# A decoder layer's conditioning products: from split fp32r weights to plain fp32 in two column strips

## The reference

```python
cs = jax.nn.silu(c)
ada = (cs @ w_ada[l] + b_ada[l]).reshape(B, N_ADA, D_MODEL)        # 1024 x 9216
h = modulate(rmsnorm(x, g_ffn1[l]), sh1, sc1)
x = x + 0.5 * gt1[:, None] * swiglu(h, w_ffn1_in[l], w_ffn1_out[l])
h = modulate(rmsnorm(x, g_mix[l]), sh2, sc2)
...
x = x + gt2[:, None] * out                                          # token mixer
h = modulate(rmsnorm(x, g_ffn2[l]), sh3, sc3)
x = x + 0.5 * gt3[:, None] * swiglu(h, w_ffn2_in[l], w_ffn2_out[l])
fin = cs @ w_ada_final + b_ada_final                                # 1024 x 2048
```

## Time and profile before

| what | value |
|---|---|
| time, median of three runs | 3044.75 us (3041.53 to 3051.48) |
| the profiled execution: span from first to last instruction | 3042.0 us |
| PE busy | 2895.1 us (95%) |
| PE weight loads busy | 2778.0 us (91%) |
| DVE busy | 1463.0 us (48%) |
| ACT busy | 867.4 us (29%) |
| mean granted TensorE clock (1 is full speed) | 0.974 |
| memory traffic | 63 GB/s over the span |

### The profile page before, as it was taken

How to read it: one execution, slowest core, us unless ns; L and a number is a source line. 1 busy time by engine, 2 the same in 40 slices (tenths; PEclk the granted TensorE clock), 3 DMA queues, 4 the chain that set the end, 5 groups by cost and what they waited for, 6 DMA issues and landing times. The chain is left out here.

```text
span 3042.0 us, 45017 instructions
## 1 busy us (share of the span) xinstructions
PE 2895.1 (95%) x17729; PEld 2778.0 (91%) x17729; DVE 1463.0 (48%) x3102; ACT 867.4 (29%) x1396; POOL 131.1 (4%) x190
## 2 busy tenths in 40 slices
PE   5899999999998989999999999999989999999997
PEld 3799999999998989889988988998889999999996
DVE  4655545444445644436345433634674443343436
ACT  5422222222213412332233233223441111111114
POOL 2000000000003010000000000000200000000002
PEclk7899999999999999999999999999999999999998
DMA  7122222222111131212111221211021111111111
GB/s 227 53 88 96 97 97 86 94 97 97 55 42 29 43 101 50 73 32 68 49 56 32 65 73 32 67 49 56 22 70 42 41 55 41 41 41 41 41 42 59
DMA packets 167528, 193.05 MB, mean 63 GB/s; under 512 B 7760, under 2 KB 157036, under 8 KB 167349
## 3 DMA queue, kind: packets, MB, share of 16 engines
q1 hardware_dynamic: 166962, 191.12, 19.7%
q10 hardware_dynamic: 342, 0.15, 0.0%
q0 software_dynamic: 96, 0.00, 0.0%
HBM read 172.38 MB, written 18.87 MB: 63 GB/s over the span
## 5 line engine op out<-in xcount | busy, mean ns | idle before, releaser
L521 DVE SCALAR_TENSOR_TENSOR xT<-ps,gate_p,xT 128x384 f32<-128x384 f32 (+1 forms) x624 | 348.3, 571 | 115.5 <-PE ps L801 97.4
L907 PE MATMUL ps<-hhi,mw_hi 128*128 128x384 f32 (+1 forms) x1152 | 392.6, 341 | 9.2 <-DVE mw_lo L1684 7.4
L908 PE MATMUL ps<-hlo,mw_hi 128*128 128x384 f32 (+1 forms) x1152 | 379.3, 329 | 0.0
L738 DVE TENSOR_TENSOR hf<-st,ps 128x384 f32<-128x384 f32 x132 | 70.2, 532 | 642.3 <-PE ps L822 640.3
L909 PE MATMUL ps<-hhi,mw_lo 128*128 128x384 f32 (+1 forms) x1152 | 378.9, 329 | 0.0
L820 PE MATMUL ps<-hhi,wa_hi 128*128 128x384 f32 (+1 forms) x1056 | 350.0, 331 | 16.9 <-DVE wa_lo L728 14.0
L821 PE MATMUL ps<-hlo,wa_hi 128*128 128x384 f32 (+1 forms) x1056 | 347.8, 329 | 0.0
L822 PE MATMUL ps<-hhi,wa_lo 128*128 128x384 f32 (+1 forms) x1056 | 347.5, 329 | 0.0
L820 PE MATMUL ps<-hhi,wb_hi 128*128 128x384 f32 (+1 forms) x1056 | 346.1, 328 | 0.1
L822 PE MATMUL ps<-hhi,wb_lo 128*128 128x384 f32 (+1 forms) x1056 | 346.0, 328 | 0.0
L821 PE MATMUL ps<-hlo,wb_hi 128*128 128x384 f32 (+1 forms) x1056 | 346.0, 328 | 0.0
(11 more groups left out here) (298 smaller groups left out, 5250.7 us busy)
## 6 DMA issues: line engine op xcount, KB each, us to landing
ada_raw<-in_w_ada SPq DMA_DIRECT2D x36, 1024.0 KB, 5.1
mw_raw<-in_w_in SPq DMA_DIRECT2D x32, 1024.0 KB, 5.7
wa_raw<-in_w_ffn_in SPq DMA_DIRECT2D x22, 1024.0 KB, 5.1
wb_raw<-in_w_ffn_in SPq DMA_DIRECT2D x22, 1024.0 KB, 5.2
wo_raw<-in_w_ffn_out SPq DMA_DIRECT2D x22, 1024.0 KB, 4.9
ada_raw<-in_w_ada_final SPq DMA_DIRECT2D x8, 1024.0 KB, 5.3
cs<-in_state_mlstm_C SPq DMA_DIRECT2D x32, 256.0 KB, 2.8
out_C_sample<-cs SPq DMA_DIRECT2D x32, 256.0 KB, 2.2
```

The costliest lines, as they stand in the source:

```text
L521: ins = dve.scalar_tensor_tensor(out=xT[:, m, t0:t0 + wp], in0=ps[:, bank, 0:wp], scalar=gate_p[:, m:m + 1], in1=xT[:, m, t0:t0 + wp], op0 ...
L738: dve.tensor_tensor(M["hf"][:, n, 0:w], M["st"][:, n, 0:w], ps[:, up_bank("b", b, i, n), 0:w], ALU.mult).then_inc(C["hidden"].sem, 1)
L907: pe.matmul(out, wh, xh, start=(j == 0), stop=False)
L908: pe.matmul(out, wh, xl, start=False, stop=False)
```

## The change

The products take the raw fp32 weights: the splits by ACT and DVE go, and with them the buffers `ada_hi` and `ada_lo`. silu(c) is kept as fp32, nine columns padded with zeros to 32 (`csT`). The eight matmuls of a group alternate between two strips of 32 columns of the array: even slices k add up in PSUM partitions 0 to 31, odd ones in 32 to 63. ACT copies 64 rows out, and the turn, before a pair of transposes, is a pair of plain fp32 matmuls against `strip_sum`, a 128 x 9 matrix of zeros and ones that adds the two strips. `ada_keep` is one operation. The memory of the split buffers serves as raw slots: ten in `bring_in` (loads 10 and 11 wait for products 0 and 1), two in `ffn`, where the load of a group waits for the product two before it.

```diff
+        ADA_FIRST, ADA_SLOTS = 12, 10
+        ada_raw = [ar.put(f"ada_raw{s}", [P, KT, 256]) for s in range(2)] + [
+            ar.put(f"ada_raw{s}", [P, KT, 256], at=hi_at + 8192 * (s - 2)) for s in range(2, ADA_SLOTS)]
+        ada_rows = ar.put("ada_rows", [P, 256])
+        strip_sum = ar.put("strip_sum", [P, 9])
+        csT = ar.put("csT", [P, KT, 32])
+        ar.at = top + 3 * 8192
...
-        def ada_high(act, turn, halves_free, slot=0, half=0):
-            act.wait_ge(*ada_in[slot](turn * 16 + 16))
-            if halves_free is not None:
-                act.wait_ge(*ada_mm(halves_free))
-            for i in range(2):
-                act.activation(ada_hi[half][:, :, 128 * i:128 * i + 128], ada_raw[slot][:, :, 128 * i:128 * i + 128],
-                               ACT.Copy).then_inc(ada_hi_done.sem, 1)
-        def ada_low(dve, g, slot=0, half=0):
-            for i in range(2):
-                c = slice(128 * i, 128 * i + 128)
-                dve.wait_ge(*ada_hi_done(g * 2 + (i + 1)))
-                dve.tensor_tensor(ada_lo[half][:, :, c], ada_raw[slot][:, :, c], ada_hi[half][:, :, c].bitcast(F32),
-                                  ALU.subtract).then_inc(ada_lo_done.sem, 1)
-        def ada_product(pe, g, half=0, reused=True):
-            pe.wait_ge(*ada_lo_done(g * 2 + 2))
+        def ada_product(pe, g, slot, turn, reused=True):
+            pe.wait_ge(*ada_in[slot](turn * 16 + 16))
             if reused:
                 pe.wait_ge(*ada_rows_kept(g))
             for k in range(KT):
-                pe.matmul(ps[0:18, 6, 0:256], cs_r[:, k, :], ada_hi[half][:, k, :], start=(k == 0), stop=False)
-                ins = pe.matmul(ps[0:18, 6, 0:256], cs_r[:, k, :], ada_lo[half][:, k, :], start=False, stop=(k == KT - 1))
+                strip = 32 * (k % 2)
+                ins = pe.matmul(ps[strip:strip + 32, 6, 0:256], csT[:, k, :], ada_raw[slot][:, k, :], start=(k < 2), stop=(k >= KT - 2))
             ins.then_inc(ada_mm.sem, 1)
         def ada_copy_rows(act, g, reused=True):
             act.wait_ge(*ada_mm(g + 1))
             if reused:
                 act.wait_ge(*ada_turned(g))
-            act.activation(ada_rows[:, :], ps[0:18, 6, 0:256], ACT.Copy).then_inc(ada_rows_kept.sem, 1)
+            act.activation(ada_rows[0:64, :], ps[0:64, 6, 0:256], ACT.Copy).then_inc(ada_rows_kept.sem, 1)
         def ada_turn(pe, g, reused=True):
             if reused:
...
             pe.wait_ge(*ada_rows_kept(g + 1))
             pe.sem_inc(ada_passed.sem, 1)
             for i in range(2):
-                ins = pe.transpose(ps[:, 7, 18 * i:18 * i + 18], ada_rows[:, 128 * i:128 * i + 128], ident[0:18, 0:18])
+                ins = pe.matmul(ps[:, 7, 9 * i:9 * i + 9], ada_rows[:, 128 * i:128 * i + 128], strip_sum[:, :], start=True, stop=True)
             ins.then_inc(ada_turned.sem, 1)
         def ada_keep(dve, g):
             dve.wait_ge(*ada_turned(g + 1))
             dst = ada[:, bass.ds(g * 2, 2), :]
-            out = ps[:, 7, 0:36].rearrange("p (j s) -> p j s", s=18)
-            dve.tensor_tensor(dst, out[:, :, 0:9], bc(bT[:, bass.ds(g * 2, 2)], 2, 9), ALU.add).then_inc(*dve_steps.one())
-            dve.wait_ge(*dve_steps.now())
-            dve.tensor_tensor(dst, dst, out[:, :, 9:18], ALU.add).then_inc(ada_kept.sem, 1)
+            out = ps[:, 7, 0:18].rearrange("p (j s) -> p j s", s=9)
+            dve.tensor_tensor(dst, out, bc(bT[:, bass.ds(g * 2, 2)], 2, 9), ALU.add).then_inc(ada_kept.sem, 1)
...
-                    for g in range(12):
-                        if g >= 4:
-                            sp.wait_ge(*ada_lo_done(2 * (g - 4) + 2))
-                        ada_load(sp, g, g % 4)
+                    for g in range(ADA_FIRST):
+                        if g >= ADA_SLOTS:
+                            sp.wait_ge(*ada_mm(g - ADA_SLOTS + 1))
+                        ada_load(sp, g, g % ADA_SLOTS)
...
-                    def high(g):
-                        ada_high(act, g // 4, g - 2 if g >= 3 else None, g % 4, g % 3)
                     for u, (t0, n) in enumerate(UNITS):
                         for k in range(1, KT, 2):
                             g = KT * u + k
                             act.wait_ge(*x_turned(g + 1))
                             act.activation(xT[:, k, t0:t0 + n], ps[:, g % 6, 0:n], ACT.Copy).then_inc(x_kept_a.sem, 1)
-                        high(u)
                         if u == 0:
                             act.wait_ge(*v_turned(1))
-                            act.activation(csT[:, :, :], ps[:, 6, 0:72], ACT.Copy).then_inc(v_kept.sem, 1)
-                            act.wait_ge(*v_kept(1))
-                            act.activation(cs_r[:, :, 0:9], csT[:, :, :], ACT.Copy).then_inc(v_kept.sem, 1)
+                            act.wait_ge(*made(5))
+                            act.activation(csT[:, :, 0:9], ps[:, 6, 0:72].rearrange("p (k s) -> p k s", s=9), ACT.Copy).then_inc(cs_ready.sem, 1)
                     act.wait_ge(*v_turned(2))
                     act.activation(bT[:, :], ps[:, 7, 0:ALL_T], ACT.Copy).then_inc(v_kept.sem, 1)
                     act.activation(vT[:, :], ps[:, 7, 128:256], ACT.Copy).then_inc(v_kept.sem, 1)
...
                     act.wait_ge(*x_kept_a(12))
                     for g in range(12):
                         ada_copy_rows(act, g, reused=g >= 1)
-                        if g < 9:
-                            high(g + 3)
                         sq.square(act, 2 * g)
                         sq.square(act, 2 * g + 1)
...
-                        ada_low(dve, u, u, u)
+                    dve.wait_ge(*made(6))
+                    dve.tensor_tensor(strip_sum[:, :], ident[:, 0:9], ident[:, 32:41], ALU.add).then_inc(made.sem, 1)
                     dve.wait_ge(*v_kept(2))
-                    dve.tensor_tensor(cs_r[:, :, 9:18], csT[:, :, :], cs_r[:, :, 0:9].bitcast(F32), ALU.subtract).then_inc(cs_ready.sem, 1)
-                    dve.wait_ge(*v_kept(4))
-                    for g in range(12):
-                        if g < 9:
-                            ada_low(dve, g + 3, (g + 3) % 4, g % 3)
-                        if g >= 1:
-                            ada_keep(dve, g - 1)
-                    ada_keep(dve, 11)
+                    for g in range(ADA_FIRST):
+                        ada_keep(dve, g)
...
-                            sp.wait_ge(*ada_lo_done(group(b, q) * 2))
-                            ada_load(sp, group(b, q))
+                            sp.wait_ge(*ada_mm(group(b, q) - 1))
+                            ada_load(sp, group(b, q), q % 2)
...
-                                ada_product(pe, group(b, 2 * i + n // 2))
+                                q = 2 * i + n // 2
+                                ada_product(pe, group(b, q), q % 2, b * 2 + (q // 2 - 2))
```

More of the change, by code:

```diff
@@ L145, in layer @@
         ar.at = top = ar.end // 32 * 32 - 4 * (RINGS * 384 + T + KT * NSEQ * STOK) - 3 * 8192
-        ada_raw = [ar.put("ada_raw0", [P, KT, 256])] + [
-            ar.put(f"ada_raw{s}", [P, KT, 256], at=hi_at + 8192 * (s - 1)) for s in range(1, 4)]
-        ada_hi = [ar.put("ada_hi0", [P, KT, 256], F32R), ar.put("ada_hi1", [P, KT, 256], F32R, at=hi_at + 3 * 8192),
-                  ar.put("ada_hi2", [P, KT, 256], F32R, at=hi_at + 5 * 8192)]
-        ada_lo = [ar.put("ada_lo0", [P, KT, 256], F32R), ar.put("ada_lo1", [P, KT, 256], F32R, at=hi_at + 4 * 8192),
-                  ar.put("ada_lo2", [P, KT, 256], F32R, at=hi_at + 6 * 8192)]
+        ADA_FIRST, ADA_SLOTS = 12, 10
[5 more added lines that the diff above has]
+        ar.at = top + 3 * 8192
         norm_at = ar.at
@@ L154, in layer @@
         rr = ar.put("rr", [P, T])
-        ada_rows = ar.put("ada_rows", [18, 256], at=ar.at)
         ts = ar.put("norm_samples", [P, KT, NSEQ, STOK])
-        ada_in = [cnt(f"ada_in{s}") for s in range(4)]
-        ada_hi_done, ada_lo_done, ada_mm, ada_rows_kept, ada_turned, ada_kept, ada_passed = (
-            cnt("ada_" + n) for n in ("hi_done", "lo_done", "mm", "rows_kept", "turned", "kept", "passed"))
+        ada_in = [cnt(f"ada_in{s}") for s in range(ADA_SLOTS)]
+        ada_mm, ada_rows_kept, ada_turned, ada_kept, ada_passed = (
+            cnt("ada_" + n) for n in ("mm", "rows_kept", "turned", "kept", "passed"))
         squared, squares_added, mean_done, rms_done, t_done, hi_done, lo_done = (
@@ L276, in bring_in @@
             crow2 = ar.put("crow2", [9, D])
-            csT = ar.put("csT", [P, KT, 9])
             brow = ar.put("brow", [ALL_T, P])
@@ L347, in _ @@
                     pool.memset(eps_col[:, :], EPS).then_inc(made.sem, 1)
-                    pool.wait_ge(*made(3))
+                    pool.memset(csT[:, :, :], 0.0).then_inc(made.sem, 1)
+                    pool.memset(ada_rows[:, :], 0.0).then_inc(made.sem, 1)
+                    pool.wait_ge(*made(5))
                     pool.affine_select(out=ident[:, :], in_=ident[:, :], compare_op=ALU.not_equal, fill=1.0,
@@ L396, in _ @@
```

(28 more changed lines are left out.)

6 lines of the change are left out of this document (1 added, 5 removed).

## The result

The changed kernel takes **3013.44 us** (median of four runs, 3009.16 to 3015.38) against 3047.23 (four runs, 3041.53 to 3051.48): a ratio of 0.9888, 95% interval 0.9868 to 0.9908, or some 34 us less. The profiled execution took 3013.23 us with a span of 3010.8 us, at a mean granted clock of 0.980.

What follows compares the result with a forecast made beforehand. PE's own work was taken to bound ffn, a chain of waits bring_in. ffn +12.8 and start -21.0 give -8.2 us on the profiled 3042.0, 3033.8; with 2.75 to the median, 3036.5 us, range 3026 to 3064.

Steps and rivals of the forecast that it cites:

- ffn, +12.8: First ffn: a group costs PE 2.79 us against 2.39, +0.40 for each of 32 groups.
- the start, -21.0: bring_in: last product starts at 63.1 us against 84.57, with a tail longer by 0.5.
- The sign named for the first: First ffn: PE busy over 719 of 720 us would confirm that ACT and DVE were covered there.
- staggered pairs: Each product: records of the two strips overlap one behind the other, 8 x 0.215 + 0.215 = 1.94 us.
- A: Each product: strips take turns, 3.44 us, a group in ffn 4.29; 3105 us in all; chance 0.18.
- B: Each product: strips overlap in part, a quarter of the hidden time comes back; 3052 us in all; chance 0.14.
- Change of shape and turn: Each group: switching matmul shapes costs 0.4 us a product; the turn takes 0.45 us against 0.43, no change.
- step (a): Start of bring_in: x's transposes no longer stop, so the first product starts at 23.5 us against 36.62.
- step (b): Rounds of bring_in: 3.3 us at full clock, 3.6 with one group in eight at the low clock.
- Rival C: bring_in: strips overlap but half stays at low clock, period 4.5 us, gain 11; 3046 us in all; chance 0.13.
- the end of -24.5: bring_in: best case of the gain, with first product at 23.3 us and rounds of 3.3 us.
- Tail: bring_in, behind the last product: longer by 0.5 us.

Runs made afterwards that it cites:

- one strip: The changed kernel with all eight matmuls of a product in columns 0 to 31 and 32 rows copied; 3086.72 us.
- same addresses: The changed kernel with an unused 576-byte pad, so later buffers lie where they lay before the change; run twice, 3021.85 and 3024.64 us.
- halves: The changed kernel with slices 0 to 3 in the first strip and 4 to 7 in the second, not alternating; 3055.40 us.
- four strips: The changed kernel with slice k in strip k mod 4, 128 rows copied and a turn that adds four strips; 2993.95 us.

## Why the prediction was wrong

It had the sign and the mechanism of each of the two stages right and missed the size of both, and it put the rest of the kernel at no change without giving a reason. In span it was 23.0 us too high (3033.8 for 3010.8). The failed steps are three terms of its sum: ffn, +12.8 where +3.2 was measured (9.6 us); the start, -21.0 where -29.05 was measured (8.1 us); and all later stages, at nothing, where -5.65 in the mixer and +0.34 behind it were measured (5.3 us).

- **What bounds.** Right. The splits were covered in ffn and on the path in `bring_in`. The sign named for the first, PE busy over 719 of 720 us, did not quite come (718.54); but PE's idle time there was only 1.65 us with the splits and 1.46 without.
- **Strips.** Right, and better than the forecast: not the staggered pairs with a first record by itself, 1.94 us, but pairs from the first record on, 8 x 0.2155 = 1.72. Rivals A and B are out: the sum of A for ffn, 4.29 us a group, is close to what one strip then cost, (87.96 - 71.19) / 4 = 4.19. Both strips use all rows, and 16 records with their loads fit into 8 steps of 0.2155, the step of one strip. The rule of the Trainium skill (TensorE: Matmul & The Clock Gate, Part 3, "What overlaps and what doesn't"), that a weight load overlaps matmuls in flight only where the row groups differ, is not borne out here. The estimate of 1.59 for two strips, worked out from the 2.38 for three column tiles that the same page of the Trainium skill gives under "Measured speedup vs the span model", did not come either: 3.57 / 1.85 is 1.93, and no run here has three strips.
- **Change of shape and turn.** From the last large matmul to a product the rows show 0.27 us instead of 0.17, and from the first large matmul behind it to the next 0.28 instead of 0.17; with the 0.13 within the product's 1.85 that is some 0.3 where 0.40 was taken. The turn, 0.36 us to the next start and 0.08 in the row behind, was forecast at 0.45. A group in ffn therefore costs (81.08 - 71.19) / 4 = 2.47 us, not 2.79, against 2.39: **+3.2 us where the sum had +12.8**. Of the 0.32 us between 2.79 and 2.47, 0.22 are the records (1.94 against 1.72), and most of the rest is the change of shape. The forecast of 82.3 for a block came out at 81.08. The term of ffn is the largest of the three misses.
- **Start, step (a).** 23.5 was forecast for the first product and 21.53 came, 2.0 us better. "48 left take 9.4 to 13.9" is where it failed: its fast end is the 4.7 us that 24 transposes took at 8.11, but the second 24 took 2.84 (at 13.19), and from there all that was left, the bias too, took 8.3, at a granted clock of 1.00.
- **Start, step (b).** This is the larger miss at the start. The period was taken as 3.6 us and measured (54.93 - 21.53) / 11 = 3.04, which is 6.2 us over eleven rounds. Half of the difference is the share of low clock, one group in eight, which did not occur: the granted clock was 1.00 up to 59 us. The rest is the product with its change of shape, 1.85 against 2.14, less a longer turn. Rival C, the low clock staying, is out. Even the end of -24.5 that the prediction kept for the start was passed (-29.05), because it held the chain at 3.3 us and the first product at 23.3 at best.
- **Tail.** Forecast +0.5 longer, measured 71.01 - 54.93 = 16.08 against 15.49: +0.6.
- **The base.** The 2.75 us between 3042.0 and 3044.75 were taken for a profiled execution below the median. Most of them are the time around the span: 3013.23 goes with a span of 3010.8, 3045.68 with 3044.0. The forecast is the same either way.
- **What the sum left out.** It followed the instructions that the change moves and took every other stage at the time it had. The change also takes the 576 bytes of `cs_r` out from below the buffers of all later stages, and the pairs of runs lie 9 to 12 us apart by it, of which the spacing of the mixer's matmuls explains 5.4. It fits the account: with equal addresses the change gives 21.9 us and 24.9 us (same addresses, two batches, against before beside them), and start and ffn alone make -29.05 + 3.16 = -25.9.

So of the 31.2 us of span about 26 are the change as described, 29 gained at the start and 3 given back in ffn, and 5.65 are the mixer's, which the place of the buffers accounts for, by the spacing of its matmuls (5.4). The timed difference of some 34 us has an interval of 28 to 40, so what it holds beyond the span's is not resolved.

## What to carry to other kernels

A small matrix product that uses few columns can have the array several times at once, in plain fp32 and without any split, if neighbouring matmuls go to different strips; use as many strips as the loads can feed: with four in `bring_in` PE waited for loads, the granted clock fell to 0.50, and the stage took 2.9 us longer than with two. Before a time is credited to an edit, run the edit at the old addresses, and the old code at the new ones: a freed table moves every later buffer. In a chain of waits, price the rounds at both clocks, and carry the full clock as a case of its own.

## What was not expected of the hardware

- In the run halves a record passes three others that are issued ahead of it and belong to another strip (2.74 us for 16 records, 12 steps of 0.2155).
- 576 bytes in the place of buffers change the spacing of the mixer's fp32r matmuls that stream 256 columns from 120.4 to 117.1 ns, while blocks of ffn without products, which stream 384 and 320 columns, go the other way by 0.03 of 71.16 us. Why, no run here shows.
- A shorter product went with a longer stage: with four strips PE was busy 59% of the 7.3 us ahead of the fall of the clock, with two 83% of the like stretch, and only the first fell to 0.50 there.
- Executions of one kernel spread by 14 us, and the mean granted clock by 0.005 to 0.006 with them.
